# Weight sums of a seven-product feed-forward moved from GpSimd to VectorE

## The reference

```python
# first block, D_FF = 3072
h = rms_norm(x, norm2_g[l])
u = depthwise_conv(h @ w_up[l], up_conv_w[l], up_conv_b[l], 1, 1)
gate, val = jnp.split(u, 2, axis=-1)
x = x + (jax.nn.gelu(gate) * val) @ w_down[l]
...
# second block, FFN_HIDDEN = 2816
h = rms_norm_2(x, norm_ffn_g[l])
gate, up = jnp.split(h @ w_ffn_in[l], 2, axis=-1)
x = x + (jax.nn.silu(gate) * up) @ w_ffn_out[l]
```

## Time and profile before

| | |
|---|---|
| median of 3 runs | 3612.82 us (3611.45 to 3614.36) |
| profiled execution, its own time | 3608.62 us |
| profiled execution, span | 3606.8 us |
| busy: PE / DVE / ACT / POOL | 94% / 59% / 40% / 33% of the span |
| stage 0, up projection | about 538 to 1048 us of the span |
| stage 1, up projection | about 2900 to 3338 us of the span |

### The profile page before, as it was taken

How to read it: one execution, slowest core, us unless ns; L and a number is a source line. 1 busy time by engine, 2 the same in 40 slices (tenths; PEclk the granted TensorE clock), 3 DMA queues, 4 the chain that set the end, 5 groups by cost and what they waited for, 6 DMA issues and landing times.

```text
span 3606.8 us, 44590 instructions
## 1 busy us (share of the span) xinstructions
PE 3402.4 (94%) x16628; PEld 2721.5 (75%) x16628; DVE 2132.4 (59%) x2137; ACT 1457.3 (40%) x1900; POOL 1190.1 (33%) x681
## 2 busy tenths in 40 slices
PE   6999997999989989999999999999889979999997
PEld 4677775777777867888877777777668768887786
DVE  7876966676773346222267888888865543333433
ACT  5687834444441133322233433443452343333213
POOL 1100026999952212111121111111112267776222
PEclk9999998999999999999999999999999989999998
DMA  2000221222233112111111111111122212123321
GB/s 108 24 1 15 74 88 45 78 80 77 81 145 138 47 41 88 35 41 35 41 48 41 37 34 41 41 35 40 41 77 81 87 47 87 70 87 116 128 87 76
DMA packets 55532, 233.03 MB, mean 65 GB/s; under 512 B 6161, under 2 KB 6161, under 8 KB 49937
## 3 DMA queue, kind: packets, MB, share of 16 engines
q1 hardware_dynamic: 55440, 231.78, 18.0%
HBM read 190.34 MB, written 41.42 MB: 64 GB/s over the span
## 4 chain that ended last, share of the span: by engine, by line
PE 73%; DVE 17%; issue 4%; ACT 4%; DMA 1%; POOL 1%; DVEq 0%; SPq 0%; POOLq 0%; ACTq 0%
PE ps L495 40%; PE ps L1284 22%; DVE conv_acc L1934 4%; PE ps L2273 2%; PE ps L2285 2%; PE ps L2262 1%; PE ps L518 1%; PE ps L2431 1%; DVE small L1974 1%; DVE t_wide L962 1%; DVE ffn_gate L1192 1%; PE ps L2418 1%; PE ps L511 1%; DVE conv_acc L1936 1%; PE ps L2370 1%
## 5 line engine op out<-in xcount | busy, mean ns | idle before, releaser
L467 POOL TENSOR_TENSOR w_lo_part<-w_raw,w_hi_part 128x1024 fp32r<-128x1024 f32 x166 | 415.0, 2500 | 1815.2 <-ACT w_hi_part L450 1815.0
L495 PE MATMUL ps<-h_hi_part,w_hi_part 128*128 128x512 f32 x1904 | 622.4, 408 | 43.9 <-DVE h_lo_part L616 29.3
L495 PE MATMUL ps<-h_lo_part,w_hi_part 128*128 128x512 f32 x1904 | 595.8, 394 | 0.0
L495 PE MATMUL ps<-h_hi_part,w_lo_part 128*128 128x512 f32 x1904 | 593.7, 393 | 0.0
L450 ACT ACTIVATE w_hi_part<-w_raw 128x1024 fp32r<-128x1024 f32 x180 | 189.3, 1051 | 737.6 <-PE ps L495 619.2
L495 PEld LDWEIGHTS ps<-h_hi_part,w_hi_part 128*128 128x128 f32 x1904 | 346.3, 190 | 138.3 <-issue 57.5
L495 PEld LDWEIGHTS ps<-h_hi_part,w_lo_part 128*128 128x128 f32 x1904 | 361.6, 190 | 78.9
L495 PEld LDWEIGHTS ps<-h_lo_part,w_hi_part 128*128 128x128 f32 x1904 | 361.9, 190 | 78.5
L1934 DVE SCALAR_TENSOR_TENSOR conv_acc<-u_pad,cols,conv_acc 128x1024 f32<-128x1024 f32 x232 | 307.4, 1325 | 20.4 <-DVE conv_acc L1934 4.6
L1844 DVE TENSOR_TENSOR residual<-residual,ps 128x1024 f32<-128x1024 f32 (+1 forms) x64 | 78.1, 1221 | 295.5 <-PE ps L495 267.1
L495 PE MATMUL ps<-u_hi,w_hi_part 128*128 128x512 f32 x736 | 229.8, 394 | 11.9 <-issue 4.9
(11 more groups left out here) (422 smaller groups left out, 6596.9 us busy)
## 6 DMA issues: line engine op xcount, KB each, us to landing
w_raw<-in_w SPq DMA_DIRECT2D x226, 512.0 KB, 3.5
w_raw_odd<-in_w SPq DMA_DIRECT2D x46, 512.0 KB, 4.0
u_spill<-ffn_u SPq DMA_DIRECT2D x46, 512.0 KB, 3.1
u_wide<-u_spill SPq DMA_DIRECT2D x23, 1024.0 KB, 9.8
residual<-in_x SPq DMA_DIRECT2D x4, 1024.0 KB, 7.9
residual<-in_x SPq DMA_DIRECT2D x2, 2048.0 KB, 7.1
x_spill<-residual SPq DMA_DIRECT2D x2, 2048.0 KB, 8.5
residual_spill<-residual SPq DMA_DIRECT2D x1, 4096.0 KB, 12.1
```

Source lines behind the costliest of these rows:

```text
L467: pool.tensor_tensor(WLO[:, slot], WRAW[:, slot], f32(WHI[:, slot]), ALU.subtract).then_inc(w_ready, 1)
L495: last = pe.matmul(PS[:, ps, b * HALF:(b + 1) * HALF], st[:, slot, k, :], at(mv, k, b), start=(k == 0 and n == 0), stop=(k == nk - 1 and n ...
```

## The change

The four sums of a pair become `up_sums(eng, m, q)`, which takes the engine. POOL still makes those of pairs 0, 1 and 2 of each stage. For every later pair DVE makes them at the end of its cycle c, for pair c+2: 21 pairs in stage 0 and 19 in stage 1. DVE waits ahead of them for the low part of `a12(c+2)`. POOL's order keeps the seven low parts and loses the sums.

```diff
-        def up_sums_pool(pool, m, q):
+        def up_sum_one(eng, m, q, n):
 
             raw = m.raw[q.odd()]
             a11, a12, a21, a22 = raw[:, 0, 0:4], raw[:, 0, 4:8], raw[:, 1, 0:4], raw[:, 1, 4:8]
-            pool.wait_ge(raw_val[q.odd()], raw_count(m, q))
-            for n, (to, a, b, op) in enumerate(((TMP[:, :, :], a21, a22, ALU.add), (a21, a21, a11, ALU.subtract),
-                                                (a11, TMP[:, :, :], a11, ALU.subtract), (a12, a12, a11, ALU.subtract))):
-                pool.tensor_tensor(to, a, b, op).then_inc(up_sum, 1)
-                pool.wait_ge(up_sum, q.lin(4, 4 * m.g + n + 1))
+            to, a, b, op = ((TMP[:, :, :], a21, a22, ALU.add), (a21, a21, a11, ALU.subtract),
+                            (a11, TMP[:, :, :], a11, ALU.subtract), (a12, a12, a11, ALU.subtract))[n]
+            if n == 0:
+                eng.wait_ge(raw_val[q.odd()], raw_count(m, q))
+            else:
+                eng.wait_ge(up_sum, q.lin(4, 4 * m.g + n))
+            if n == 1:
+                eng.wait_ge(raw_gate[q.odd()], raw_count(m, q))
+            eng.tensor_tensor(to, a, b, op).then_inc(up_sum, 1)
+
+        def up_sums(eng, m, q):
+            for n in range(4):
+                up_sum_one(eng, m, q, n)
...
             def cycle(c):
                 for op, q in (("s2", 1), ("s3", 1), ("a11", 2), ("a12", 2)):
                     up_lo_pool(pool, m, op, c + q)
-                up_sums_pool(pool, m, c + 2)
+                if first(c):
+                    up_sums(pool, m, c + 2)
                 for op, q in (("s1", 2), ("a22", 1), ("s4", 1)):
                     up_lo_pool(pool, m, op, c + q)
...
-            def cycle(c):
+            def cycle(c, more=True):
                 scaled(c + -1)
                 gate_taps(c + -1)
                 if not m.conv:
@@ -1249,9 +1258,12 @@
                 c11(c + 1)
                 if m.conv:
                     made(c + -1)
+                if more:
+                    dve.wait_ge(up_lo, split_at("a12", c + 2) + m.steps)
+                    up_sums(dve, m, c + 2)
 
             up_cycles(dve, m, cycle, st, 6 if m.conv else 0)
-            cycle(At(n - 2))
+            cycle(At(n - 2), False)
```

More of the change, by code:

```diff
@@ L841, in up_pool @@
                 up_lo_pool(pool, m, op, At(0))
-            up_sums_pool(pool, m, At(0))
+            up_sums(pool, m, At(0))
             for op, q in (("s1", 0), ("s2", 0), ("a11", 1), ("s3", 0), ("a12", 1)):
                 up_lo_pool(pool, m, op, At(q))
-            up_sums_pool(pool, m, At(1))
+            up_sums(pool, m, At(1))
             for op, q in (("s1", 1), ("a22", 0), ("s4", 0)):
```

## The result

| | before | after |
|---|---|---|
| median of 4 runs each | 3612.14 us (3607.46 to 3614.36) | 3637.15 us (3635.21 to 3639.12) |
| profiled execution, span | 3606.8 us | 3636.8 us |
| DVE / POOL busy, share of the span | 59% / 33% | 62% / 26% |

The account below looks back on a forecast made before the run. Stage 0 was taken as bound by a chain of each pair's matmuls and then DVE, 20.0 us per pair, not by POOL. The terms +12.7, +18.9 and -5.3 sum to +26.3 us, so 3639.1, range 3615 to 3653.

Parts of the forecast that it names:

- Stage 1, +12.7: Stage 1: s4's low part on POOL meets L1192 and lengthens it, 0.67 us in each of 19 pairs, +12.7 us.
- Stage 0, +18.9: Stage 0: DVE's sums come too late because of turns with POOL, 0.9 us in each of 21 pairs, +18.9 us.
- The walk: One stage 0 period from a11, DVE and POOL taking turns: fourth sum ends at 18.25 us, PE starts at 20.85.
- the choice between 0.85 and 1.1 per pair: Stage 0: +0.85 us per pair if POOL goes first at 6.5, +1.1 if DVE does; 0.9 was taken.
- The new wait: DVE's wait for a12's low part ahead of the sums, in both stages; predicted to cost nothing.
- Stage 0's end, -5.3: End of stage 0: s4's low part done earlier, so SP's last loads and the store go earlier; -5.3 us.
- PE's clock, priced at nothing: Stage 0: PE's gaps grow from 0.6 to 1.6 us per pair; no loss of clock was priced.
- One sign that the prediction gave for being wrong: In either stage, L1192 showing 0.70 us would mean that the forecast is wrong.
- the 1.35 to 1.42 named: Stage 1: the predicted sign that L1192 takes 1.35 to 1.42 us, with the period at about 20.0.
- B: Stage 0: the sums fit in time, costing 2 us there; +9.5 us in all, 3622; 20 in 100.
- D: Stage 1 is spared as L1192 slips ahead of POOL, stage 0 as forecast; +14 us, 3626; 7 in 100.
- A: Stage 0: POOL no longer blocks L1192, period falls to 19.4; -18 us with the stage's end, 3595; 8 in 100.

Follow-up runs that it names:

- e5: The changed kernel, with POOL waiting in stage 1 for L1201's signal before s4's low part; 3626.1 us, ratio 1.0045.
- e2: The kernel before, with the sums moved to DVE in stage 1 only, using the rewritten helper; 3616.8 us, ratio 1.0019.
- e7: The kernel before with only the rewritten helper of the sums, all sums staying on POOL; 3616.7 us, ratio 1.0016.
- e1: The kernel before, with the sums moved to DVE in stage 0 only, using the rewritten helper; 3635.6 us, ratio 1.0072.
- e6: The changed kernel, with POOL's low parts in stage 0 held back until DVE has made the four sums; 3621.8 us, ratio 1.0038.
- e8: The kernel before, with stage 0's sums moved to DVE and the old helper kept on POOL in stage 1; 3624.7 us, ratio 1.0039.
- e9: The changed kernel, with pair 3's sums of stage 0 also on POOL; 3639.9 us, ratio 1.0075.
- e4: The kernel before, with DVE's read of c21 put ahead of the other operations of `scaled`; 3606.7 us, ratio 0.9993.
- e3: The changed kernel, with DVE's read of c21 put ahead of the other operations of `scaled`; 3582.8 us, ratio 0.9923.
- e10: The changed kernel with c21 read first and pair 3's sums of stage 0 also on POOL; 3586.0 us, ratio 0.9930.

## Why the prediction was right, point by point

Forecast 3639.1, measured 3637.15; the verdict (slower) and the mechanism hold. By its steps:

1. **Stage 1, +12.7.** Measured +11.7, and e5 shows it to be s4's low part meeting L1201: without the meeting it is +0.6. The forecast's size per pair was 0.67, read from one pair with L1192 at 0.70. The pairs alternate: 19.34 and 19.46 us before, 20.10 and 19.93 now, with L1201 at 1.34 and 1.26. The means are 19.40 and 20.02, so a pair costs 0.62, and 19 of them 11.8.
2. **Stage 0, +18.9.** The steady part was a little over-sized and the start missing. The walk gave L1188 at 18.25 us behind a11, and L1197 starts at 875.51 - 857.29 = 18.2, where a11 starts at 857.29. It had the first sum end at 14.0, the third at 16.6 and a22's low part at 17.7; they ended at 14.0, 16.6 and 17.75.
   - *The order.* What failed is the choice between 0.85 and 1.1 per pair: I took 0.9, supposing that DVE first at 6.5 would make all one tap later. Both orders occur in turn (in the chain above POOL's low part of 738.97 takes 2.33 us; at 718.26 it is DVE's tap that does), and the pairs are 20.77 and 20.83 us apart. With POOL first, a12's low part goes ahead of the product L1226, as in the walk, and the sums begin 13.2 us behind a11. With DVE first, L1226 comes ahead of a12's low part, DVE idles 1.19 us for it, and the sums begin at 13.3 all the same. So it is 0.80, and 16.8 in 21 pairs.
   - *The new wait.* The prediction said that the wait for a12's low part costs nothing. It is in the chain in every second pair, and the walk's time came out right there because the product had gone ahead.
   - *The start was not foreseen.* From the first a11 behind sums by DVE to the second it is 23.2 us (626.06 to 649.26); the same two were 19.9 apart before (619.76 to 639.70), and 626.06 itself is 3.5 late beyond the shift of 2.8 that the stage begins with. From there to the last a11 the 19 periods are 15.6 longer (395.27 against 379.65). 3.5 + 3.3 + 15.6 = 22.4, where the step had 18.9; the wait (4.06, before 0.37) is what the 3.5 are, and the fall of the clock behind it some 2.4 of the 3.3 (twelve matmuls, 0.2 us more each).
3. **Stage 0's end, -5.3.** PE's last a11 (1044.53, 1019.35 before) is 25.2 us later, the last L1197 (1087.9, 1067.9) 20.0: -5.2. With step 2 that is 22.4 - 5.2 = +17.2, the stage's whole difference. The loads and the store behave as said. No experiment took this term by itself, but it goes with the place of stage 0's sums: the time between its last two reads by L1188 (L1197) is 31.7 us before, 31.6 in e2 and 32.1 in e7, which make them on POOL, and 26.6 in the change and in e1, e5, e6, e8 and e9. With c21 first it is 35.9 in e4 and 27.2 in e3 and e10.
4. **PE's clock, priced at nothing.** Right for the steady gaps of 1.3 us (1.00), wrong for the one of 4.06.

**Where it was luck.** The measured parts, 11.7 + 17.2 = 28.9, and the +30.0 of the spans belong to the profiled pair; the medians are 25.0 apart. The forecast of +26.3 lies 3.7 below the spans' difference and 1.3 above the medians'. Steps 1 and 2 were over-sized by 1.0 and 2.1 in the steady pairs, which made up for part of the missing start. So that the number came this close is in part luck; the mechanism is not.

**The signs.** One sign that the prediction gave for being wrong has come: L1201, the L1192 of before, shows 0.68 in stage 0. The sign contradicts the prediction's own walk, in which L1192 "follows without a wait", and the walk is what the trace shows. In stage 1 L1201 is at 1.34 and 1.26, a little under the 1.35 to 1.42 named. A wait on the sum before costs less than the 0.14 us that the prediction took: unblocked sums start 0.72 to 0.73 apart (858.85, 859.57, 860.30 and 861.03 in e6).

Of the rivals, B (the sums fit, 3622) is what e6 makes (3621.8), with a22's low part in s4's place and one collision left. D's case (stage 1 spared, 3626) is what e5 and e8 make (3626.1, 3624.7). A (the lock opens) wanted L1192 free because s4's low part starts late. In stage 0 L1201 is free at 0.68, but because that low part starts early, 0.31 us ahead of L1197 (875.20), and A's gain does not come: the sums, now DVE's, are late by more than L1192 had lost. In stage 1 POOL, with less to do, stands in the way more, not less (1.34). The Trainium skill ("SBUF — State Buffer", Who interferes with whom) says that issue order, not the shape of the operation, decides who is blocked. The traces agree: a lead of 0.02 us (872.03 against 872.05) made the third sum take 1.84 us instead of the 0.69 of e6, and one of 0.08 us made L1201 take 1.76 in e1.

**Noise.** The stretch between the stages, which no edit touches, took 1864 to 1870 us in all of these profiles but e5's, where it took 1860, and e5's profiled execution lies 9 us under its own median. Stage 0 with one and the same code (the change, e1, e5, e8) took 484.5 to 488.0. Nearly all of this spread lies at its start: the first wait of PE behind DVE's sums is 4.06, 4.02, 2.67 and 2.63 us, and 12, 11, 8 and none of the matmuls behind it are slow. From the next a11 to the last one the four agree within 0.2 us (395.1 to 395.3). So the 0.8 us per pair is well above the noise, and differences of 3 us of a whole stage are not read.

## What to carry to other kernels

Where two engines exclude each other by instruction, moving work from the busy to the idle one needs a walk through one period, instruction by instruction, up to the read that the bound engine waits for; busy shares did not show which instruction would be late. Such a read is best put ahead of anything that can be made to wait: with c21 first the same move is worth 24 us (3606.7 to 3582.8) instead of costing 25. And a helper that is rewritten on the way is a change of its own: measure it alone.

## What was unexpected of the hardware

```profile
622.00:624.00 2.00, 2.00 (x6) 1.56 (x5) 1.85 (x2) 0.29 (x1) 1.77 (x2) 0.50 0.44 72
...
622.00:624.00 2.00, 1.87 (x8) 1.57 (x9) 1.60 (x2) 1.97 (x2) 1.77 (x2) 1.00 0.22 37
```
